# Two 64 x 64 products on the state per head in a recurrence become one 64 x 128 product

## The reference, cut to what matters

```
def step(S, inp):
    r_t, w_t, k_t, v_t, a_t, b_t = inp
    sa = jnp.einsum('bhij,bhj->bhi', S, a_t)
    S = S * w_t[:, :, None, :] + sa[..., None] * b_t[:, :, None, :] + v_t[..., None] * k_t[:, :, None, :]
    return S, jnp.einsum('bhij,bhj->bhi', S, r_t)
```

## Time and profile before

| what | value |
|---|---|
| median of 3 runs | 2465.71 us (2463.49 to 2465.9) |
| the profiled execution's own time | 2463.49 us |
| its span, first to last instruction | 2461.7 us |
| mean granted TensorE clock | 0.949 |
| PE busy, weight loads busy | 87 %, 74 % of the span |
| DVE, ACT, POOL busy | 54 %, 34 %, 49 % |
| chain that ended last, by engine | PE 53 %, DVE 7 %, POOL 4 %, ACT 3 %, issue 8 % |

### The profile page before, as it was taken

How to read it: one execution, slowest core, us unless ns; L and a number is a source line. 1 busy time by engine, 2 the same in 40 slices (tenths; PEclk the granted TensorE clock), 3 DMA queues, 4 the chain that set the end, 5 groups by cost and what they waited for, 6 DMA issues and landing times.

```text
span 2461.7 us, 58402 instructions
## 1 busy us (share of the span) xinstructions
PE 2153.2 (87%) x23126; PEld 1818.5 (74%) x23126; DVE 1328.2 (54%) x1932; ACT 832.2 (34%) x2187; POOL 1202.8 (49%) x708
## 2 busy tenths in 40 slices
PE   6799999989999999986948989999894999797876
PEld 4699899978888888866948947777793776565654
DVE  6766666664666666654274314454316172548645
ACT  1623233335566665642122223333202111212331
POOL 1366666643233322328746702321683897765234
PEclk8899999999999999987969999999996999899998
DMA  2234334455334433332202210000122321221001
GB/s 89 88 138 146 138 146 148 161 153 119 65 74 89 89 81 66 77 97 89 93 27 70 93 43 35 34 19 33 52 85 72 99 87 39 66 69 59 18 0 69
DMA packets 158914, 197.69 MB, mean 80 GB/s; under 512 B 120992, under 2 KB 123296, under 8 KB 156448
## 3 DMA queue, kind: packets, MB, share of 16 engines
q1 hardware_dynamic: 158752, 195.25, 26.4%
HBM read 156.24 MB, written 38.99 MB: 79 GB/s over the span
## 4 chain that ended last, share of the span: by engine, by line
PE 53%; issue 8%; DVE 7%; POOL 4%; ACT 3%; POOLq 1%; DVEq 0%; ACTq 0%
PE wide L1235 9%; PE wide L1236 8%; PE wide L1237 8%; PE wide L803 8%; PE wide L1712 5%; PE wide L1821 2%; PE wide L1597 1%; PE wide L1777 1%; PE wide L1805 1%; PE wide L2074 1%; POOL x_w L1094 1%; DVE normed L1373 1%; ACT odd_probs L2317 1%; POOL n_levels L1088 1%; PE wide L828 1%
## 5 line engine op out<-in xcount | busy, mean ns | idle before, releaser
L1235 PE MATMUL wide<-mixed_high,w_high_rwkv_in 128*128 128x264 f32 x720 | 211.8, 294 | 29.3 <-ACT log_decay L435 20.4
L1094 POOL TENSOR_TENSOR x_w<-n,masks 128x192 f32<-128x192 f32 x48 | 28.7, 598 | 364.1 <-ACT n L971 364.1
L1237 PE MATMUL wide<-mixed_high,w_low_rwkv_in 128*128 128x264 f32 x720 | 206.2, 286 | 0.0
L1352 DVE TENSOR_TENSOR sq_sum<-sq_sum,squares 128x528 f32<-128x528 f32 (+1 forms) x54 | 87.3, 1617 | 183.5 <-ACT squares L1317 183.5
L1236 PE MATMUL wide<-u_low_second,w_high 128*128 128x512 f32 x464 | 185.6, 400 | 0.0
L1259 POOL TENSOR_TENSOR w_high<-weights,con 128x1024 fp32r<-128x1024 f32 x60 | 147.4, 2456 | 74.5 <-PE wide L1237 64.6
L355 PE MATMUL wide<-mixed_in,weights 128*128 128x264 f32 x672 | 158.8, 394 | 13.7 <-DVE mixed_in L325 12.3
L1235 PEld LDWEIGHTS wide<-mixed_high,w_high_rwkv_in 128*128 128x128 f32 x720 | 137.8, 191 | 37.6 <-ACT log_decay L435 26.6
L1262 POOL TENSOR_TENSOR w_low<-weights,w_high 128x1024 fp32r<-128x1024 f32 x60 | 157.6, 2627 | 4.7
L355 PEld LDWEIGHTS wide<-mixed_in,weights 128*128 128x128 f32 x672 | 128.9, 193 | 41.0 <-issue 9.5
L531 POOL TENSOR_TENSOR w_high_rwkv_in<-weights,con 128x1024 fp32r<-128x1024 f32 x45 | 108.1, 2403 | 71.4 <-PE wide L1237 70.7
(11 more groups left out here) (329 smaller groups left out, 6543.4 us busy)
## 6 DMA issues: line engine op xcount, KB each, us to landing
weights<-in_stream SPq DMA_DIRECT2D x200, 512.0 KB, 3.5
forms<-form SPq DMA_DIRECT2D x16, 2020.5 KB, 6.3
forms_in<-forms SPq DMA_DIRECT2D x96, 144.0 KB, 4.5
forms_in<-forms SPq DMA_DIRECT2D x32, 288.0 KB, 4.5
gate_bonus<-forms SPq DMA_DIRECT2D x16, 576.0 KB, 4.3
r_ahat_r<-forms SPq DMA_DIRECT2D x32, 144.0 KB, 3.7
mixed<-gate_bonus SPq DMA_DIRECT2D x14, 264.0 KB, 2.1
gated<-mixed SPq DMA_DIRECT2D x14, 264.0 KB, 4.2
```

The source lines that it names most:

```text
L1235: pe.matmul(dst, w[0], x[0], start=start, stop=False)
L1237: return pe.matmul(dst, w[1], x[0], start=False, stop=stop)
L1352: dve.tensor_tensor(sq_sum[:, 0:width], sq_sum[:, 0:width], sq[:, slot, 0:width], ALU.add).then_inc(sq_added, 1)
```

## The change

L818 and L820 become one product per head. Its weights are the two neighbouring tiles of `r_ahat_r`, 64 rows by 128 columns, and it fills all 128 rows of the head's bank at once. For the upper head these are the tiles a, r (own rows, other rows), for the lower head r, a. The waits before, L822 behind, the operands and the results are as they were.

```diff
                         pe.wait_ge(q["s_rows"], (NC - 1) * p + c)
                         for hd, rows in enumerate(HEAD_ROWS):
-                            pe.matmul(out_bank[hd][rows, block], r_a_r[rows, pw, c, 1, :], state[rows], start=True, stop=False)
-                        for hd, rows in enumerate(HEAD_ROWS):
-                            pe.matmul(out_bank[hd][OTHER_ROWS[hd], block], r_a_r[rows, pw, c, 2 - 2 * hd, :], state[rows], start=True, stop=False)
+                            pe.matmul(out_bank[hd][:, block], r_a_r[rows, pw, c, 1 - hd:3 - hd, :], state[rows], start=True, stop=False)
                     for hd, rows in enumerate(HEAD_ROWS):
                         pe.matmul(out_bank[hd][rows, block], xw[rows, W_OF + pw, c * C:(c + 1) * C], mv[rows, pw, c, :],
                                   start=c == 0, stop=True).then_inc(u_mm[hd], 1)
```

## The result

The changed kernel takes 2485.82 us (median of 5), beside 2465.71 us for the kernel before in the same measurement: a ratio of 1.009, 95 % interval 1.0077 to 1.0104. Halving the number of products on the state made the kernel about 20 us slower. The prediction was 2489 us, within 2470 to 2508. Of all executions in this document one stands apart, 6821.94 us in the last kernel, and it has no part in that kernel's ratio.

What follows compares the result with a forecast made beforehand. Stage B was taken as mostly bound by PE, 31.63 of 33.65 us per pass. The profiled 2463.5 us plus 23.4 for 15 passes at 1.56, plus 2.2 to the median, gave 2489 us, range 2470 to 2508.

Steps and rivals of the forecast that it cites:

- A change of shape costs 0.15 us each way: PE's weight loads, stage B: each shape change waits for an empty array, 0.20 us between loads, 0.15 above the unit.
- Two pairs of 128 columns, 0.11 us each: Inside the new block: its two pairs of 128-column weight loads start 0.11 us apart.
- Leaving with 64 columns costs 0.26: From the new block's last pair of loads to L822's first: 0.26 us, against 0.42 behind L861.
- The old L820 was nearly free: Old block: L820 lies beside its neighbours in other array quarters; L818 and L820 together cost only 0.11 us.
- Chunk 1 is free: Step behind L861, of the new block's own shape: 0.53 us to L822 before and after, so no change.
- 1.56 us per pass: Full stage B pass: seven steps at 0.40, 2.8 us, less 0.26, 0.18, 0.40 and 0.40 hidden in PE's waits.
- Pass 1: First pass of stage B, counted among the 15 full passes at 1.56 us each.
- Pass 16 is covered by POOL: End of stage B: POOL's 32.5 us before stage C covers pass 16; uncovered, it would cost 1 to 3 us.
- The sum: Whole kernel: 15 passes at 1.56 us, 23.4 us more than the profiled 2463.5, plus 2.2 to the median: 2489 us.
- Nothing is hidden: Rival, stage B: the waits behind the steps move along, 2.8 us per pass, 42 us in all, 2508; chance 0.14.
- Only chunks 4 and 6 pay: Rival, stage B: only these two steps reach the pass's end, 0.8 us per pass, 12 us, about 2478; chance 0.12.
- The two ways of no cost: Rivals on the block: fewer records save 14 us, 2452, chance 0.07; array sees no shape change, time unchanged, chance 0.05.

Runs made afterwards that it cites:

- the last kernel: Kernel before, with L828 and L831 split into 64*64 products, v halves started in part 0, r tile moved to part 1: 2463.71 us against 2468.26, ratio 0.9978.
- the 128*64 kernel: Kernel before, its four products per step reading all 128 rows, still 64 columns, output not the reference's: 2493.04 us against 2468.43, ratio 1.0109.
- the doubled block: Changed kernel with every merged product issued twice in a row: 2504.91 us against 2464.2 for the kernel before, ratio 1.0174.
- the kernel of chunks 2, 5 and 7: Kernel before, with the merged product in chunks 2, 5 and 7 alone, all 16 passes: 2474.16 us against 2468.43, ratio 1.0024.
- the kernel of chunks 3, 4 and 6: Kernel before, with the merged product in chunks 3, 4 and 6 alone: 2483.42 us against 2468.43, ratio 1.0070.

## Why the prediction held, step by step

The mechanism and its parts came out as worked out, but that the total was so near is partly luck: the terms that were off had different signs.

- **A change of shape costs 0.15 us each way.** Shown: 0.20 us from the last 64*64 load to L818, and 0.57 us for the block, as predicted; the 128*64 kernel has 0.58 us without any wider load. The loads show the time; that the array runs empty in it is the reading that fits, and was not tested by itself.
- **Two pairs of 128 columns, 0.11 us each.** Shown by the doubled block, 0.22 us longer.
- **Leaving with 64 columns costs 0.26.** From L818's first load to the product behind it is 0.37 us, and 0.11 of that is the second pair.
- **The old L820 was nearly free.** Supported: moving it changes nothing, on PE or in the time.
- **Chunk 1 is free.** Shown: 0.58 against 0.53 us on PE, and an unchanged pass when it alone is merged.
- **1.56 us per pass.** The quiet pass grew by 1.42 us. From the starts of L822 and its successor in two quiet passes, counted from item A, the delay is 0.06 us at chunk 1, then 0.40, 0.54, 0.75, 1.12, 1.12, 1.52 and 1.52 at chunk 8. A step adds 0.40 and the wait behind it takes a part back: 0.26 behind chunk 2, 0.18 ahead of chunk 4, all of it behind chunks 5 and 7 (so chunks 6 and 8 start from 0.72 and 1.12), as the account had it. The waits shrank as forecast: over the regular passes L803 waits 6.9 us for ACT's `e` (`PEld wide L803 <- ACT e L981: 6.9, 14, 0.6`) where it was 11.8, and the 3.2 us for DVE's `x_w` are gone from the waits view. Left out was a small wait behind chunk 8: the delay ends at 1.42.
- **Pass 1.** Taken as a regular pass, it grew by 2.4 us. This was too low, since without post-processing nothing hides chunks 5 and 7. Consistent with that, it grew by 1.7 us when only 2, 5 and 7 were merged.
- **Pass 16 is covered by POOL.** Half wrong. POOL's work does cover the start of stage C, and it even became 1.85 us shorter. But the splits of the last pairs on DVE and ACT come behind pass 16, and the first tile waited 2.1 us for them. The net of it is about 1.2 us. Pass 16 itself grew by more than the 1 to 3 us given for it: from the product of chunk 0 to that of chunk 8 it is 24.9 us, against 21.6 in the kernel that undoes the change there and 21.1 before. PE works there at a granted clock of 0.50 (windows view, 1120 to 1136 us), and the forecast had taken its prices from rows at 1.00.
- **The sum.** Passes 1 to 15 gave 18.5 us where 23.4 were predicted. The quiet passes come in two lengths, odd and even passes in turn: 33.65 and 34.23 us before, 35.08 and 35.65 after, 1.42 more for both. That is 2 us of the miss. The largest part, 3.9 us, is what stands above the quiet length in passes 2 to 15: 4.9 us in all before (with passes of 35.3, 35.0 and 35.5 us), 1.1 after. Pass 1 went the other way by 0.8. Outside passes 1 to 15 the parts listed above add up to 2.8 us, and they brought the total nearer to the forecast. The 1.5 us before any walk and the 1.1 behind the first tile of stage C are among them, and no mechanism of the change is known for either.

The rivals are settled as follows. "Nothing is hidden" (2.8 us per pass) fell with the kernel of chunks 2, 5 and 7. "Only chunks 4 and 6 pay" (0.8 us) fell with the kernel of chunks 3, 4 and 6, whose pass grew by 0.97 us. The two ways of no cost fell with the 0.57 us of the block.

## What to carry to other kernels

Count a small product by the distance between the starts of neighbouring weight loads, and ask which shape stands before and behind it. Joining two products saves nothing if they ran in separate quarters, and it lost 0.40 us here where the joined one has another shape than its neighbours, 0.3 of it for the two changes of shape; the same product is free beside work of its own shape. When a delay is spread over a pipeline, go from wait to wait and ask whether the releaser itself was delayed, and treat the first and last passes separately, since the waits that hide things there are others.

## What the runs showed of the hardware that was not expected

PE stands still at irregular places in stage B for 0.3 to 1.2 us with no releaser in the profile, as here before the change:

```profile
653.71 0.39 PE L803 MATMUL wide<-x_w,e 64*64 64x64 f32 x7 [1.06 <-issue]
```

The wait of L803 for "issue" in the regular passes is 9.6 us before, 3.9 after the change, and 13.7 in the last experiment, whose PE list is the longest. Not all of it is irregular. In each of the 14 passes L803 shows 0.23 us behind the 64*128 loads ahead of chunk 2, in all these kernels, and before the change also the 0.18 us behind chunk 2 that the new block fills. Without these, about 3.9 us are irregular before and 0.7 after, and single gaps reach 1.7 us in the last experiment. This goes with the excess of the long passes, 4.9 and 1.1 us, and so with the mean pass growing by 1.15 us and the quiet one by 1.42. Whether the gaps depend on the number of PE's instructions was not tried: each figure is from one profiled execution, and the doubled kernel, with as many products as the one before, has 3.6 us in all, nearly all of it the regular 0.23.
